# Attention probabilities scaled by a product with a diagonal matrix that also transposes them

## The reference

```python
# B: the 128 best keys by an index score are kept, the others masked
logits = einsum('bqhd,bqkhd->bqhk', qb, k_sel) * d ** -0.5
p = softmax(where(valid, logits, MASK_VALUE), axis=-1)
out = einsum('bqhk,bqkhd->bqhd', p, v_sel)
# D: causal, with a cumulated forget gate added
logits = einsum('bqhd,bshd->bhqs', qb, kh) * d ** -0.5 + cb - c
p = softmax(where(key_pos <= q_pos, logits, MASK_VALUE), axis=-1)
out = einsum('bhqs,bshd->bqhd', p, vh)
```

## Time and profile before

| what | value |
|---|---|
| median of 3 executions | 2177.32 us (2177.28 to 2185.11) |
| profiled execution | 2177.14 us, its span 2175.3 us |
| PE busy | 2036.3 us, 94% of the span |
| DVE, ACT, POOL busy | 943.5, 764.0, 1006.7 us |
| the four attentions, start to end | 44.7, 47.1, 43.7, 47.2 us |

### The profile page before, as it was taken

One profiled execution on the slowest core, in us unless ns is written; L12 is line 12 of the kernel. 1 busy time (PEld: TensorE's weight loads), 2 busy tenths in 40 slices (PEclk: granted clock), 3 DMA queues, 4 the chain that ended last, 5 costly groups with the idle time before them and its releaser, 6 DMA issues.

```text
span 2175.3 us, 31563 instructions
## 1 busy us (share of the span) xinstructions
PE 2036.3 (94%) x10760; PEld 1601.3 (74%) x10760; DVE 943.5 (43%) x1690; ACT 764.0 (35%) x1178; POOL 1006.7 (46%) x1231
## 2 busy tenths in 40 slices
PE   7999897999999899999899998979999989999995
PEld 5876755878777688888678776567786767888884
DVE  5737856323322513223177478652333315133143
ACT  6334253223542522222363342431244334122224
POOL 4444424212646555557534443422135574455574
PEclk9999998999999999999899999999999999999998
DMA  4122211001222222222212222110011222222222
GB/s 168 69 78 78 78 50 39 30 30 39 69 75 82 78 97 96 96 96 97 79 56 79 87 73 74 48 31 30 30 59 59 78 88 78 97 96 96 96 97 97
DMA packets 50352, 161.72 MB, mean 74 GB/s; under 512 B 5280, under 2 KB 13600, under 8 KB 49952
## 3 DMA queue, kind: packets, MB, share of 16 engines
q1 hardware_dynamic: 49056, 157.05, 21.9%
q10 hardware_dynamic: 1152, 2.86, 0.4%
HBM read 157.79 MB, written 2.10 MB: 73 GB/s over the span
## 4 chain that ended last, share of the span: by engine, by line
issue 54%; POOL 41%; PE 3%; POOLq 1%; DVE 1%; DMA 0%; ACT 0%; SPq 0%; DVEq 0%; ACTq 0%
POOL w_lo L1406 20%; POOL w_lo L1436 16%; POOL slab L1426 2%; PE bank L551 1%; PE bank L553 1%; PE bank L552 1%; POOL rstd L1415 1%; POOL slab L1447 1%; POOLq L1433 0%; POOL slab L1429 0%; DMA w_raw<-wproj 0%; DVE u_lo L1505 0%; POOLq L1402 0%; DVE u_hi L1516 0%; DVE u_lo L1517 0%
## 5 line engine op out<-in xcount | busy, mean ns | idle before, releaser
L1406 POOL TENSOR_TENSOR w_lo<-w_raw,w_hi 128x256 fp32r<-128x256 f32 x624 | 500.6, 833 | 819.4 <-ACT w_hi L1046 819.1
L551 PE MATMUL bank<-hn_hi,w_hi 128*128 128x512 f32 x1312 | 550.8, 420 | 43.6 <-POOL w_lo L1406 21.1
L1436 POOL TENSOR_TENSOR w_lo<-w_raw,w_hi 128x256 fp32r<-128x256 f32 x512 | 379.9, 774 | 303.3 <-ACT w_hi L1366 303.3
L552 PE MATMUL bank<-hn_lo,w_hi 128*128 128x512 f32 x1312 | 518.2, 395 | 0.0
L553 PE MATMUL bank<-hn_hi,w_lo 128*128 128x512 f32 x1312 | 517.8, 395 | 0.0
L551 PEld LDWEIGHTS bank<-hn_hi,w_hi 128*128 128x128 f32 x1312 | 250.4, 191 | 125.3 <-issue 51.9
L551 PE MATMUL bank<-u_hi,w_hi 128*128 128x512 f32 x736 | 298.6, 406 | 24.0 <-POOL w_lo L1398 11.4
L553 PEld LDWEIGHTS bank<-hn_hi,w_lo 128*128 128x128 f32 x1312 | 250.0, 191 | 54.6
L552 PE MATMUL bank<-u_lo,w_hi 128*128 128x512 f32 x736 | 288.6, 392 | 0.0
L553 PE MATMUL bank<-u_hi,w_lo 128*128 128x512 f32 x736 | 288.6, 392 | 0.0
L1366 ACT ACTIVATE w_hi<-w_raw 128x1024 fp32r<-128x1024 f32 x128 | 135.8, 1061 | 429.5 <-DMA w_raw<-wrest 404.2
(11 more groups left out here) (313 smaller groups left out, 2695.6 us busy)
## 6 DMA issues: line engine op xcount, KB each, us to landing
w_raw<-wrest SPq DMA_DIRECT2D x144, 512.0 KB, 3.3
w_raw<-wmerge SPq DMA_DIRECT2D x80, 512.0 KB, 3.5
w_raw<-wproj SPq DMA_DIRECT2D x64, 512.0 KB, 3.5
x<-x_in SPq DMA_DIRECT2D x4, 512.0 KB, 7.1
slab<-rope ACTq DMA_DIRECT2D x2, 1024.0 KB, 4.8
out<-x SPq DMA_DIRECT2D x4, 512.0 KB, 2.6
con<-tables SPq DMA_DIRECT2D x1, 898.0 KB, 11.3
slab<-masks SPq DMA_DIRECT2D x1, 896.0 KB, 12.9
```

Of the source, the lines that this page charges most:

```text
L551: mm(o_, stat[0], mov[0], start=first, stop=False)
L552: mm(o_, stat[0], mov[1], start=False, stop=False)
L1406: ins = pool.tensor_tensor(wlo[:, s_, cs], wraw[:, s_, cs], whi[:, s_, cs].bitcast(f32), SUB)
L1436: ins = pool.tensor_tensor(wlo[:, s_, cs], wraw[:, s_, cs], whi[:, s_, cs].bitcast(f32), SUB)
```

## The change

Before, DVE multiplied the row of probabilities (128, 256, 384 or 512 wide) by the reciprocal of the row sum, and PE transposed the result with its transpose instruction. Now DVE multiplies the 128x128 identity by the same reciprocals, which gives a diagonal matrix in one of four new places (`scales`, in the slab's part 3). PE then runs an ordinary fp32 product: the unscaled probabilities are the operand that stands in the array, the diagonal matrix moves through it, and what comes out is the scaled and transposed tile. From step 4 on, DVE waits for `probs_transposed` of the step that used the same place before.

```diff
+        scales = [slab[:, 3, i * P:(i + 1) * P] for i in range(4)]
...
                         for j in range(i // H + 1):
-                            ins = pe.transpose(ps[6][:, j * P:(j + 1) * P], S(6 + i % 4 // 2, i % 2)[:, j * P:(j + 1) * P],
-                                               C("ident"))
+                            ins = mm(ps[6][:, j * P:(j + 1) * P], S(6 + i % 4 // 2, i % 2)[:, j * P:(j + 1) * P], scales[i % 4],
+                                     start=True, stop=True)
                         ins.then_inc(*at_tr.up())
...
                     def probs(i):
-                        n = (i // H + 1) * P
-                        buf = S(6 + i % 4 // 2, i % 2)[:, 0:n]
                         dve.wait_ge(*at_ex.at(L, base + i + 1))
                         link(dve.reciprocal(col[:, 6, i % 4:i % 4 + 1], col[:, 2, i % 4:i % 4 + 1]))
-                        ts(buf, buf, col[:, 6, i % 4:i % 4 + 1], None, MUL).then_inc(*at_p.up())
+                        if i >= 4:
+                            dve.wait_ge(*at_tr.at(L, base + i - 3))
+                        ts(scales[i % 4], C("ident"), col[:, 6, i % 4:i % 4 + 1], None, MUL).then_inc(*at_p.up())
```

## The result

| | before | changed |
|---|---|---|
| median | 2177.30 us (4 runs, 2176.67 to 2185.11) | 2199.92 us (4 runs, 2191.22 to 2203.09) |
| ratio (of the means) | | 1.0089, 95% interval 1.0050 to 1.0129 |
| profiled execution, span | 2177.14, 2175.3 us | 2191.22, 2189.4 us |

The changed kernel is slower. The forecast was 2190.5 us with a range up to 2197; the profiled execution is within a microsecond of the forecast, the median lies 9.4 us above it and 2.9 us above the range. By the ratio of the means it would be 2177.3 x 1.0089 = 2196.7 us, just inside. So there are two things to explain: the 14 us between the profiled executions, and why other executions of the same kernel take 12 us more.

A forecast was written before the change was run, and what follows sets the result against it. PE was taken as the bound nearly everywhere; 2 x 4.4 us (D) plus 2 x 2.2 us (B) gave 13.2 us on 2177.14, or 2190.3, and 2190.5 us with the runs' median 0.2 higher; range 2184 to 2197 us.

The forecast's parts named there:

- Direction, place and mechanism: Four attentions: 0.6% slower; PE busy throughout D (second of a layer), mostly in B (first); each fp32 product two records.
- 0.11 us a tile, 4.4 us a D: On PE, a tile costs 0.22 in place of 0.11 us; 40 tiles add 4.4 us to each second attention (D).
- one record: Rival for the new products on PE: each goes as one record of 0.11 us, not slower, 2176 us; chance 0.07.
- four times the transpose's price: Rival for the new products on PE: 0.44 us a tile, 46 us more in all, 2224 us; chance 0.03.
- the load is no dearer a pace than the product: PE's weight loads: four such records' loads take 0.52 us, those of four transposes 0.59, so loads add nothing.
- B, 2.2 us: First attention of a layer: 4.4 us added on PE, partly hidden in waits for DVE, leaves it 2.2 us later.
- the waits at steps 6 and 8: In B, PE's waits of 0.62 and 0.78 us for DVE absorb the added tiles; lateness 0 after step 8's wait.
- step 14 gain 0.4 us from the shorter scaling: In B, DVE's scaling before PE's 1.35 us wait falls from 0.93 to 0.55 us, gaining 0.4; lateness then 1.36.
- the extra wait instruction, priced at 0 to 0.05 us: On DVE, 12 in each attention, semaphore always met already; cost between nothing and 0.05 us.
- The rival that B hides all: B hides its whole share through DVE's slack, only D pays 8.8 us: 2186.1 us; chance 0.15.
- The sum, 13.2 us: All four attentions: 2 x 4.4 us in D plus 2 x 2.2 us in B, added to the profiled 2177.14 us.
- the granted clock a microsecond or two: First tiles of B run at half the granted clock; that stretch's length moves the time by a microsecond or two.

The follow-up runs named there:

- only_d: Against the kernel before, the change in the D attentions (second of each layer) alone, B (first) as before: 2184.86 us, ratio 1.0035.
- only_b: Against the kernel before, the change in the B attentions (first of each layer) alone, D (second) as before: 2184.93 us, ratio 1.0036.
- twice: The kernel before with each transpose issued twice into the same place, DVE's scaling as before: 2201.99 us, ratio 1.0090 to the kernel before.
- half_cols: The changed kernel with only 64 of the diagonal matrix's 128 columns moving through: 2198.46 us, ratio 1.0096 to the kernel before.
- no_wait: The changed kernel without DVE's second wait before the scaling: 2194.41 us, ratio 1.0103 to the kernel before.

## Why the prediction was right or wrong

- **Direction, place and mechanism: right.** PE bounds D and most of B, the fp32 product goes as two records, and nothing behind an attention takes the delay up. only_d and only_b show the places, twice the mechanism.
- **0.11 us a tile, 4.4 us a D: right within 4%.** It is 0.1145 and 4.58; the plain doubling of transposes gives 4.41. The rivals of one record and of four times the transpose's price fell.
- **That the load is no dearer a pace than the product: right.** I saw the two keep step. half_cols shows that the load alone holds 0.11 us a record, and the first two records of a step show that the 128 columns of an fp32 product would take 0.108 us by themselves.
- **B, 2.2 us: mis-sized, 2.75 measured.** The step that failed is DVE's part. I let the waits at steps 6 and 8 hide all of PE's delay but nothing more, and step 14 gain 0.4 us from the shorter scaling. At step 8 the changed kernel is 0.09 to 0.17 us late instead of 0, because the extra wait instruction, priced at 0 to 0.05 us, costs 0.1. At step 14 the scaling took 0.63 us instead of 0.55 and the wait lost 0.65 us instead of 0.84. The tiles, at 0.1145 us instead of 0.11, make up the rest. That `no_wait` is 2.15 us over before, as I had forecast, is luck: it is 0.37 us ahead at step 8, where I had 0, and loses that again behind it. The rival that B hides all fell.
- **The sum, 13.2 us: 14.6 at an equal mean clock, 14.1 between the profiled executions.** Of the 1.5 us missing to the attentions' 14.7, 0.4 are D's size and 1.1 B's.
- **The median: too low, by the clock.** I gave the granted clock a microsecond or two, and only for the first tiles of B. Three executions of the kernel before, two of them equal to 0.04 us, had looked like a quiet kernel; with 75 more they run from 2170 to 2195 us. The first four executions of the changed kernel held two at 0.967, and these lifted the median past the range's end; the other two, at 0.974 and 0.973, took 2191.2 and 2196.8 us.

## What to carry to other kernels

Scaling folded into a transposing product is not free on PE: in fp32 it loads the tile twice, and costs what two transposes cost. Fold work into the engine that bounds the kernel only if what it takes off another engine ends a wait; here PE waited 2.75 us in a B for DVE, and the change added 4.6 to PE. Where the mean clock moves from execution to execution, compare stages of the traces at one clock level before reading a ratio of medians. Times at an equal mean clock are a second check, here good to 2 or 3 us.

## What the runs showed of the hardware that I had not expected

- A 128-wide fp32 or fp32r weight load paces small products at 0.11 us, whether 64 or 128 columns move through (D 51.54 and 51.59 us) and whether the type needs one record or two (47.08 us with one). The columns of an fp32 record take as long: where the load is ahead, the next record starts after 0.108 us with 128 columns, 0.055 with 64, and 0.060 with 128 in fp32r.
- A wait instruction whose semaphore was met long before costs DVE 0.1 us between two short instructions (gap of 0.134 against 0.035 us).
- The same program on the same chip varies by 1% with PE's mean granted clock (32 executions of the kernel before: 0.978 to 0.966, 2170.4 to 2194.6 us), at about 1.75 us for each 0.001, and stretches at the lower level appear in one execution and not in another (450 to 475 us, granted clock 1.00 and 0.66).
